# A transformer block kernel: the opening up to the first projection is put in another order

## What is computed

```python
def rms_norm(x, g):
    xf = x.astype(jnp.float32)
    y = xf * lax.rsqrt(jnp.mean(xf * xf, axis=-1, keepdims=True) + NORM_EPS)
    return (y * g.astype(jnp.float32)).astype(x.dtype)
...
mod_x = (silu_c @ w_mod[i] + b_mod[i])[:, None, :]
mod_c = silu_cc @ w_mod[i] + b_mod[i]
sh_x, sc_x, g_x = jnp.split(mod_x, 3, axis=-1)
sh_c, sc_c, g_c = jnp.split(mod_c, 3, axis=-1)
hx = rms_norm(x, norm_g[i]) * (1.0 + sc_x) + sh_x
hc = rms_norm(ctx, norm_g[i]) * (1.0 + sc_c) + sh_c
...
k = px[..., A_WIDTH:A_WIDTH + A_KV_WIDTH]   # px = hx @ w_in
kc = rms_norm(pkv[..., :A_KV_WIDTH] ...)    # pkv = hc @ w_in[:, ...]
```

## Time and profile before

| | us |
|---|---|
| median of 3 runs | 1624.19 (1623.81 to 1627.51) |
| the profiled execution's own time | 1623.98 |
| its span, first to last instruction | 1622.2 |
| TensorE busy | 1534.7 (95% of the span) |
| VectorE, ScalarE, GpSimd busy | 754.4, 640.9, 688.1 |
| mean granted clock of TensorE | 0.978 of full |

### The profile page before, as it was taken

How to read it: one execution, slowest core, us unless ns; L and a number is a source line. 1 busy time by engine, 2 the same in 40 slices (tenths; PEclk the granted TensorE clock), 3 DMA queues, 4 the chain that set the end, 5 groups by cost and what they waited for, 6 DMA issues and landing times.

```text
span 1622.2 us, 25653 instructions
## 1 busy us (share of the span) xinstructions
PE 1534.7 (95%) x10114; PEld 1244.3 (77%) x10114; DVE 754.4 (47%) x1733; ACT 640.9 (40%) x1339; POOL 688.1 (42%) x660
## 2 busy tenths in 40 slices
PE   5999999999899999999998899999999989999997
PEld 3887777777688788787876687878787867766875
DVE  4444555555532534534355454733432564455253
ACT  4234444444532533433334353434332344443331
POOL 2534444443432533433325444535255434444462
PEclk8999999999999999999999999999999999999998
DMA  9111111110233222322321222222131221111221
GB/s 396 44 67 38 42 53 53 53 53 28 72 100 128 78 72 82 108 79 79 105 92 43 100 85 78 79 68 88 52 104 53 92 91 53 53 53 53 94 88 52
DMA packets 22438, 129.80 MB, mean 80 GB/s; under 512 B 2480, under 2 KB 2608, under 8 KB 8368
## 3 DMA queue, kind: packets, MB, share of 16 engines
q1 hardware_dynamic: 22176, 127.92, 22.8%
q10 hardware_dynamic: 144, 0.26, 0.1%
HBM read 126.08 MB, written 2.10 MB: 79 GB/s over the span
## 4 chain that ended last, share of the span: by engine, by line
PE 80%; DVE 9%; ACT 3%; POOL 3%; issue 3%; DMA 1%; SPq 0%; POOLq 0%; DVEq 0%; ACTq 0%
PE PS L1463 15%; PE PS L1465 15%; PE PS L1464 15%; PE PS L1586 6%; PE PS L1561 6%; PE PS L1544 4%; PE PS L1458 3%; PE PS L1459 3%; PE PS L1460 3%; PE PS L1551 3%; DVE sm L2170 2%; PE PS L1639 1%; PE PS L1631 1%; PE PS L1476 1%; DMA XC<-in_xt 1%
## 5 line engine op out<-in xcount | busy, mean ns | idle before, releaser
L2493 POOL TENSOR_TENSOR WL<-W,WH 128x512 fp32r<-128x512 f32 x304 | 400.4, 1332 | 330.9 <-ACT WH L1742 330.6
L1463 PE MATMUL PS<-HX,WH 128*128 128x512 f32 x1008 | 420.3, 417 | 11.8 <-DVE LX L2083 3.9
L1465 PE MATMUL PS<-HX,WL 128*128 128x512 f32 x1008 | 399.1, 396 | 0.0
L1464 PE MATMUL PS<-LX,WH 128*128 128x512 f32 x1008 | 398.2, 395 | 0.0
L1463 PEld LDWEIGHTS PS<-HX,WH 128*128 128x128 f32 x1008 | 193.1, 192 | 62.0 <-issue 17.1
L1465 PEld LDWEIGHTS PS<-HX,WL 128*128 128x128 f32 x1008 | 192.0, 190 | 42.6
L1464 PEld LDWEIGHTS PS<-LX,WH 128*128 128x128 f32 x1008 | 192.7, 191 | 35.8 <-issue 2.6
L1742 ACT CAST WH<-W 128x512 fp32r<-128x512 f32 x320 | 186.8, 618 | 42.0 <-PE PS L1460 25.6
L1830 ACT ACTIVATE AR<-PS,sm 128x768 f32<-128x768 f32 (+4 forms) x160 | 115.7, 723 | 165.2 <-DVE sm L2175 93.7
L2170 DVE TENSOR_REDUCE sm<-PS 128x1 f32<-128x512 f32 (+4 forms) x224 | 149.9, 669 | 43.7 <-PE PS L1551 39.3
L2560 POOL TENSOR_SCALAR AR<-AR,sm 128x768 f32<-128x768 f32 (+1 forms) x96 | 77.1, 804 | 186.2 <-DVE sm L2186 186.0
(11 more groups left out here) (290 smaller groups left out, 2546.3 us busy)
## 6 DMA issues: line engine op xcount, KB each, us to landing
W<-in_wu SPq DMA_DIRECT2D x98, 1024.0 KB, 4.9
AR<-in_wu SPq DMA_DIRECT2D x8, 1024.0 KB, 11.1
AR<-in_biasb SPq DMA_DIRECT2D x32, 256.0 KB, 2.7
XX<-in_xt SPq DMA_DIRECT2D x2, 1024.0 KB, 6.2
out<-XX SPq DMA_DIRECT2D x8, 256.0 KB, 2.2
XX<-in_xt SPq DMA_DIRECT2D x2, 768.0 KB, 5.3
XC<-in_xt SPq DMA_DIRECT2D x1, 1024.0 KB, 14.2
C<-in_cc SPq DMA_DIRECT2D x1, 770.5 KB, 8.7
```

Source lines behind the costliest of these rows:

```text
L1463: e.matmul(o, wh, xh, start=(k == 0), stop=False)
L1464: e.matmul(o, wh, xl, start=False, stop=False)
L1465: t = e.matmul(o, wl, xh, start=False, stop=(k == 7))
L2493: e.tensor_tensor(WL[:, d, a:z], W[:, n % 2, a:z], WH[:, d, a:z].bitcast(F32), ALU.subtract).then_inc(*s_wl_pool.by(n, q))
```

## The change

What it does, part by part:

- SyncE loads x in three pieces (two blocks, two blocks, four blocks) and issues nothing more until the first has landed; the unit W 0 is issued ahead of XC.
- The sums of squares of the context are taken by GpSimd (L2570 after the change), in the plan behind the first two pieces of W 0's low part, which GpSimd now makes too (`helped`). ScalarE writes the eight squares to places of their own (`apart`) and waits for none of the adds.
- The single units 0 and 1 are used and turned ahead of the spread of x's norm, and nothing of the context stands ahead of them.
- The loop is written out: keys of x for blocks 0 and 1 stand behind the use of unit 2, those of blocks 2 and 3 behind unit 4, and so on; one single unit stands between two pieces of keys where two stood.
- The context's blocks are normed later and in groups (3, 2, 3), the high part by ScalarE and the low part by GpSimd in a step of its own (`ctx_low`), and the keys of the context stand two to four blocks behind those of x: blocks 0 and 1 ahead of x's 4 and 5, blocks 2 and 3 ahead of x's 6 and 7, and the last four blocks at the end.
- `Unit("ak", whole=False)`: the keys may start before all four pieces of W 0 are split.

The arithmetic and the number of instructions of each kind stay the same, but for one more load. Behind the opening the order on every engine is the same as before.

```diff
-                split_by[n, q] = "pool" if n > 1 and not quick[0] else "dve"
+                split_by[n, q] = "pool" if (n > 1 or helped[0]) and not quick[0] else "dve"
...
+            def __init__(self, *key, whole=True):
...
-                while any(m <= n for m, _ in pieces):
+                while whole and any(m <= n for m, _ in pieces):
...
         do("early", 1)
+        load(0)
         do("context_load")
-        load(0)
         for n in range(2, 8):
...
-        norm("a", ar, X_CTX, (), lambda k, p: [(s_x[2], (2,)) if p else (s_x[k // 4], (k // 4,))])
+        norm("a", ar, X_CTX, (), lambda k, p: [(s_x[3], (3,))] if p else [(s_x[min(k // 2, 2)], (min(k // 2, 2),))])
+        norms["a"].apart = hb0
...
         norm_sums("a", 0, FIRST)
         next(first[0])
         do("norm_rs", "a", 0)
+        next(first[1])
         WIDE.take("RA", (s_scaled, (0, 7)), (s_rc, (0,)))
-        rbroad("a", 0, PS[:, 0:1024])
-        for k in range(KC):
-            do("square", "a", k, 1)
-        next(first[1])
-        norm_sums("a", 1, FIRST)
+        rdiag("a", 0)
+        split(0)
+        helped[0] = True
+        tick(True)
+        tick(True)
+        helped[0] = False
         run(first[0])
         run(first[1])
+        rspread("a", 0, PS[:, 0:1024])
         for m in range(2):
             for j in range(2):
                 Order.hold(("ak", m, j), (4 + 2 * m + j,), [(s_kraw, (m,))])
-        split(0)
-        for n in range(0, 8, 2):
+        un = Unit("ak", whole=False)
+
+        def first_scale(n):
             do("gain", 0, n)
-            modulate_x(0, n)
-            if n == 0:
-                do("norm_rs", "a", 1)
-                tick(True)
-            modulate_x(0, n + 1)
-            if n < 6:
-                next(first[n + 2])
-                next(first[n + 3])
-            if n == 0:
-                rbroad("a", 1, PS[:, 0:1024])
-                do("scale_ctx", 0)
-                un = Unit("ak")
-            else:
-                keys_rows(1, [n - 2, n - 1])
-            do("scale_ctx_k", 0, n)
-            do("scale_ctx_k", 0, n + 1)
-            if n < 6:
-                run(first[n + 2])
-                run(first[n + 3])
-            keys_rows(0, [n, n + 1])
-        keys_rows(1, [6, 7])
+            do("scale", 0, n)
+            do("scale", 0, n + 1)
+            do("scale_low", 0, n)
+            do("scale_low", 0, n + 1)
+
+        def ctx_norm(*ks):
+            for k in ks:
+                do("ctx_norm", k)
+
+        def ctx_keys(*ks):
+            for k in ks:
+                do("ctx_low", k)
+            keys_rows(1, ks)
+
+        for k in range(KC):
+            do("square", "a", k, 1)
+        first_scale(0)
+        next(first[2])
+        keys_rows(0, [0, 1])
+        next(first[3])
+        tick(True)
+        run(first[2])
+        run(first[3])
+        norm_sums("a", 1, MODS)
+        do("gain", 0, 2)
+        do("scale", 0, 2)
+        do("scale", 0, 3)
+        do("norm_rs", "a", 1)
+        next(first[4])
+        rbroad("a", 1, PS[:, 0:1024])
+        do("scale_ctx", 0)
+        do("scale_low", 0, 2)
+        do("scale_low", 0, 3)
+        ctx_norm(0, 1, 2)
+        tick(True)
+        keys_rows(0, [2, 3])
+        next(first[5])
+        run(first[4])
+        run(first[5])
+        first_scale(4)
+        next(first[6])
+        ctx_keys(0, 1)
+        ctx_norm(3, 4)
+        tick(True)
+        keys_rows(0, [4, 5])
+        next(first[7])
+        run(first[6])
+        run(first[7])
+        first_scale(6)
+        ctx_keys(2, 3)
+        ctx_norm(5, 6, 7)
+        tick(True)
+        tick(True)
+        keys_rows(0, [6, 7])
+        ctx_keys(4, 5, 6, 7)
...
-                if k > 2:
-                    w.wait_ge(*s_acc(name, k - 2, p))
-                o = N.acc if k == 0 else N.sq[(k - 1) % 2]
+                if p and N.apart:
+                    o = N.acc[:, lo:hi] if k == 0 else N.apart.at(k, lo, hi)
+                else:
+                    if k > 2:
+                        w.wait_ge(*s_acc(name, k - 2, p))
+                    o = (N.acc if k == 0 else N.sq[(k - 1) % 2])[:, lo:hi]
                 scale = 1.0 if N.gain is None else v(N.gain, k, k + 1)
-                e.activation(o[:, lo:hi], xT.at(k, lo, hi), ACT.Square, scale=scale).then_inc(*s_sq.by(name, k, p))
+                e.activation(o, xT.at(k, lo, hi), ACT.Square, scale=scale).then_inc(*s_sq.by(name, k, p))
...
+            def square(name, k, p):
+                N = norms[name]
+                if k and p and N.apart:
+                    lo, hi = 128 * N.parts[p][0], 128 * N.parts[p][1]
+                    w.wait_ge(*s_sq(name, k, p))
+                    if k > 1:
+                        w.wait_ge(*s_acc_pool(name, k - 1, p))
+                    e.tensor_tensor(N.acc[:, lo:hi], N.acc[:, lo:hi], N.apart.at(k, lo, hi), ALU.add).then_inc(*s_acc_pool.by(name, k, p))
+
+            def ctx_norm(k):
+                a, h, shift = scaled[0][0], scaled[0][4].at(k, T, NT), mod[0][:, k, 1:2]
+                w.wait_ge(*s_rc(0))
+                w.wait_ge(*s_acc_pool("a", 7, 1))
+                e.tensor_tensor(h, xT.at(k, T, NT), Rc, ALU.mult).then_inc(*s_normed_ctx.by(0, k))
+                w.wait_ge(*s_gain(0, k | 1))
+                w.wait_ge(*s_normed_ctx(0, k))
+                e.tensor_scalar(h, h, a[:, k, 1:2], shift, ALU.mult, ALU.add).then_inc(*s_scaled_ctx.by(0, k))
+
+            def ctx_low(k):
+                w.wait_ge(*s_xh("a", k, 1))
+                e.tensor_tensor(L.at(k, T, NT), scaled[0][4].at(k, T, NT), H.at(k, T, NT).bitcast(F32), ALU.subtract).then_inc(*s_xl_pool.by("a", k, 1))
...
-                for i in range(2):
-                    e.dma_start(XX[:, 2048 * i:2048 * i + 2048], xt[:, 2048 * i:2048 * i + 2048]).then_inc(*s_x[i].by(i))
+                for i, (a, b) in enumerate(((0, 1024), (1024, 2048), (2048, 4096))):
+                    e.dma_start(XX[:, a:b], xt[:, a:b]).then_inc(*s_x[i].by(i))
+                w.wait_ge(*s_x[0](0))
                 e.dma_start(C[:, :], cc).then_inc(*s_c.by())
```

More of the change, by code:

```diff
@@ L266, in build @@
         s_v, s_c, s_cs, s_pos, s_out = (signal(n, 16) for n in ("vectors", "consts", "rope_table", "positions", "stored"))
-        s_x = [signal(f"x{i}", 16) for i in range(3)]
+        s_x = [signal(f"x{i}", 16) for i in range(4)]
         s_w = [signal(f"unit{i}", 16) for i in range(2)]
@@ L350, in build @@
         loaded, unit_end, split_by, split_prev, started = set(), {}, {}, {}, set()
-        pieces, quick, used, part_last = [], [False], [0], [None, None]
+        pieces, quick, helped, used, part_last = [], [False], [False], [0], [None, None]
         groups = {}
@@ L469, in build, with added @@
             sums: object
+            apart: object = None
+            def added(self, name, k, p):
+                return (s_acc_pool if p and self.apart else s_acc)(name, k, p)
         norms = {}
@@ L492, in rbroad, with rdiag, rspread @@
         def rbroad(name, p, o):
+            rdiag(name, p)
+            rspread(name, p, o)
+        def rdiag(name, p):
+            for i in range(*norms[name].parts[p]):
+                dg_prev[name, i], dg_last[i % 4] = dg_last[i % 4], (name, i)
+                do("rdiag", name, i)
+        def rspread(name, p, o):
             rbout[name] = o
             for i in range(*norms[name].parts[p]):
-                dg_prev[name, i], dg_last[i % 4] = dg_last[i % 4], (name, i)
                 do("rbroad", name, i)
@@ L1490, in norm_sums @@
                 w.wait_ge(*s_c())
-                w.wait_ge(*s_acc(name, 7, p))
+                w.wait_ge(*N.added(name, 7, p))
                 lo, hi = N.parts[p]
@@ L1772, in scale @@
                 e.activation(H.at(k, 0, T), hb.at(k, 0, T), ACT.Identity, bias=mod[l][:, k, 0:1]).then_inc(*s_xh.by(phase, k, 0))
-            def scale_ctx_k(l, k):
-                a, Rb, rb, perm, hb, phase, first = scaled[l]
-                w.wait_ge(*s_scaled_ctx(l, k))
-                e.copy(H.at(k, T, NT), hb.at(k, T, NT)).then_inc(*s_xh.by(phase, k, 1))
+            def ctx_norm(k):
+                w.wait_ge(*s_scaled_ctx(0, k))
+                e.copy(H.at(k, T, NT), scaled[0][4].at(k, T, NT)).then_inc(*s_xh.by("a", k, 1))
             def low_ctx_k(l, k):
@@ L1997, in x_gb @@
                 e.activation(sgb[2 * j + m], groups["gb", j, m].out, ACT.Tanh, scale=0.5).then_inc(*s_gbt.by(2 * j + m))
-            program(e, w, dict(silu=silu, split=split, mod_row=mod_row, square=square, scale_ctx=scale_ctx, scale_ctx_k=scale_ctx_k, low_ctx_k=low_ctx_k, scale=scale,
+            program(e, w, dict(silu=silu, split=split, mod_row=mod_row, square=square, scale_ctx=scale_ctx, ctx_norm=ctx_norm, low_ctx_k=low_ctx_k, scale=scale,
                                parts=parts, a_key_raw=a_key_raw, a_key_rope=a_key_rope, a_query_raw=a_query_raw, a_query_high=a_query_high, a_gate=a_gate, score_exp=score_exp,
@@ L2026, in square @@
```

(6 more changed lines are left out.)

21 lines of the change are left out of this document (6 added, 15 removed).

## The result

| | before | changed |
|---|---|---|
| median of 7 runs each, us | 1624.29 (1622.61 to 1627.51) | 1629.82 (1627.40 to 1631.37) |
| ratio, with its 95% interval | | 1.0027 [1.0017, 1.0037] |
| span of the profiled execution | 1622.2 | 1628.6 |
| first matmul of the values, the mark | 62.94 | 67.70 |
| TensorE busy ahead of the mark | 42.27 | 44.96 |

By the ratio the change costs 4.4 us on 1624.19, that is 1628.6 (the medians of the table lie 5.5 apart): just inside "no change", and near the upper end of the range. The change is slower all the same: at the mark the sum gave 0.4, and it is 4.76. Of those, 2.07 are idle time of TensorE and 2.69 the same matmuls taking longer.

A forecast was written before the change was run, and what follows sets the result against it. Bound by TensorE's unchanged work, so only opening waits and clock level count: 1623.98 plus 0.4 at the first values' matmul gives 1624.4, plus 0.3 for GpSimd beside VectorE gives 1624.7 us; range 1619.5 to 1629.5.

The forecast's parts named there:

- the sum: Opening's steps added up to the first values' matmul: 63.3 against 62.94, so 0.4 us slower.
- Where it goes: From first keys to values: lead of 7.1 us shrinks to 2.8 at keys 2 and 3, values at 63.3.
- The loads: Start of the opening: x's last half lands at 8.9, adds end at 12.7 instead of 13.11, gain 0.4 us.
- Holding back the constants costs nothing: Load queue at the start: waiting for x's first piece costs 0, since the constants' bytes come behind x's anyway.
- Up to the first keys: Opening up to keys 0 and 1: they start at 25.1, 7.1 us sooner; GpSimd's adds run 22.1 to 27.9.
- The way to keys 2 and 3: Chain from unit 3 through context's sums and VectorE's diagonals: keys 2 and 3 start at 37.7, 4.3 us sooner.
- Unit 5 44.1, row 44.5, turn 44.8, scaling at 45.6: Hand-offs between keys 2, 3 and keys 4, 5: scaling starts 1.5 us after unit 5 ends.
- The clock: TensorE's low level behind idle time: keys 2 and 3 take 5.4 us, last keys 2.9 plus 1.8.
- What no row shows: GpSimd adding while VectorE makes the first two low parts: VectorE waits at most 0.73 us, 0.3 taken.
- Rival 1: Opening's gaps close: 1620.4 with the high clock, 1617.4 (6.5 us sooner) without waits; chance beyond 4.9 us 0.14.
- Rival 2: GpSimd's adds end late, at 35.7, holding up TensorE's context sums: 7.1 us slower, 1631.1; chance with like delays 0.10.
- Rival 3: Loading x alone at first gains nothing: the 0.4 us goes, 1625.1; counted inside the forecast, no separate chance.

The follow-up runs named there:

- splits_late: Changed kernel with three split pieces issued behind unit 6 instead of ahead of unit 5's row; ratio 1.0005 to the kernel before.
- x_two_wait: Changed kernel with x loaded in two halves, later loads still waiting for the first half to land; ratio 1.0008 to the kernel before.
- adds_vector: Changed kernel with the context's seven adds on VectorE behind the first low parts instead of on GpSimd; ratio 1.0023 to the kernel before.
- late_x_two_fill: Changed kernel with x in two halves, no wait, three splits behind unit 6, and 20 useless matmuls in two TensorE idle places; ratio 0.9982 to the kernel before.
- before_fill: Kernel before with 22 useless matmuls in two of TensorE's idle places; ratio 0.9997 to the kernel before.
- before_x_three: Kernel before with x loaded in three pieces and a wait for the first ahead of other loads; ratio 1.0022 to the kernel before.
- clock_fill: Changed kernel with 32 useless matmuls of 256 columns in four of TensorE's idle times; ratio 1.0008 to the kernel before.
- late_x_two: Changed kernel with x in two halves, no wait, and three split pieces behind unit 6; ratio 0.9990 to the kernel before.

## Why the prediction was where it was

The verdict (within 0.3%, and no gain) came out, but barely, with a centre 4 us too low, and an interval that reaches to 0.37%. Of the signs, the first square (5.37), the first keys and the chain to keys 2 and 3 came as said. The values did not: I had 61 to 65, and 67.70 is just short of the 68 beyond which I had called the mechanism wrong. No set of keys took the full 5.4 either; two ran nine of their twelve at 0.43 and took 4.8. At the mark I had 63.3 and it was 67.70. By the steps of "Where it goes" these 4.4 are:

| stretch | predicted | measured | missing |
|---|---|---|---|
| start to keys 2, 3 | 37.7 | 38.36 | 0.7 |
| keys 2, 3 and unit 5 | 6.4 | 5.07 | -1.3 |
| end of unit 5 to keys 4, 5 | 3.8 | 7.80 | 4.0 |
| keys 4, 5 and unit 7 | 3.9 | 3.84 | -0.1 |
| end of unit 7 to keys 6, 7 | 3.8 | 4.96 | 1.2 |
| keys 6, 7, context's last four | 7.7 | 7.67 | 0.0 |

The 1.3 that keys 2 and 3 gave back is luck of the clock in this execution: they took 4.1 here and 5.3 in splits_late.

- **"The loads" failed.** Its step was "by the rate it lands 2.45 after 6.4, at 8.9", with the 429 GB/s of the earlier trace rows, a window in which larger pieces ran. It landed at 10.24, at 340 to 360 GB/s, and the adds ended at 14.0, not 12.7. "Gain here: 0.4" was a loss of 0.9. "Holding back the constants costs nothing" failed too, as far as the profiles go: x_two_wait has unit 2 at 24.54 against 23.13, and the changed kernel at 24.69 against 24.38 without its wait.
- **"Up to the first keys"** was right in kind: keys at 26.55 against 25.1, late by what the loads were late. The adds ran from 23.01 to 29.5 against 22.1 to 27.9, beside it as said.
- **The way to keys 2 and 3** held, link by link: context's sums 34.25 (32.9), keys 38.36 (37.7), released by VectorE's diagonal.
- **"Unit 5 44.1, row 44.5, turn 44.8, scaling at 45.6" is the step that failed most.** It counted the row's copy and the turn, and left out what the plan puts ahead of them on ScalarE and VectorE: three casts (1.65) and three pieces of WL (2.66). The row was copied 1.9 after unit 5's end and the scaling began 4.7 after it, where I had 1.5. The diff shows one of them (`tick(True)` ahead of `keys_rows(0, [2, 3])`), the order of VectorE all three. The sum has no term for them. That is 3.2 of the 4.0. The other 0.8 is the clock again: "unit 6 and the context's keys 0 and 1 (2.5) lie in this gap", and they took 4.1, past the first low part. The 2.3 from the first scaling to the low part held (48.14 to about 50.4). Of the 1.2 missing ahead of keys 6 and 7, 0.8 lie between unit 7's end and the first scaling (57.38, 2.3 behind it and not 1.5), and 0.4 in the low parts.
- **The clock** was right in sum. I had the low level for all of keys 2 and 3 and it ended after five of them (5.4 became 4.1), and three quarters of the last ones (4.7, measured 4.8). That keys behind such an idle time run at the low level held in part: of the nine kernels of the table that have no useless matmuls ahead of keys 6 and 7, and idle 1.84 to 2.53 there, six took 4.4 to 4.8 for them and three 3.2.
- **"What no row shows"**: I took 0.3, between nothing and one add of 0.73; that VectorE waits at most one add was my estimate, and no run shows the 0.3. adds_vector shows nothing in the time (1.0023 against 1.0027, the intervals overlap). VectorE's first two low parts did take 0.48 longer beside the adds, 1.89 together where adds_vector has 1.41, which is less than one add of 0.73, and unit 2 covered it. The prediction did not look at the other end of the opening: the low parts of blocks 6 and 7, for which the last keys wait, took 2.11 beside GpSimd's context work, where those of blocks 4 and 5 took 1.42. What that is worth was not tried.
- **Rival 1** fell in the changed kernel: the gaps did not close. late_x_two_fill is the nearest to what it describes, with two parts of the change taken back and useless work put in, and gains 1.9 at the mark where it said up to 6.5.
- **Rival 2** fell: the adds ended at 29.5, ahead of the sums. Its result, a loss of some microseconds, came from another place.
- **Rival 3** was right that x alone at first gains nothing, and too mild: it costs.
- Of **the 1.5 us at 110 to 120** nothing was in the prediction, which let the mark set the end. It does not come with the change alone: that turn stands 56.7 to 56.9 behind the mark in the changed kernel and ten of the variants, before_fill and before_x_three among them, and 55.3 in the kernel before, clock_fill and late_x_two_fill. What decides at which level the keys behind the scores run was not tried. It also makes the 6.4 between the two profiled executions more than the 4.4 of the ratio.

Still open: how late_x_two's other ten runs look at the mark; by the time they are 1.6 us under the kernel before. Why x's 512 KB pieces load slower in six of seven executions was not taken further than their size, nor was it tried why unit 2's weights come 1.2 us later with three pieces and no wait. Whether the change's other parts, W 0 ahead of the context or the context's groups, gain or cost was not tried one by one.

## What to carry to other kernels

When a step is moved, list what every engine issues between the link before and the link behind it, and price the queue, not the link alone: here three splits that nobody needed yet cost 3.6 us in a change that lost 4.4. A load cut into smaller pieces is to be priced from a row of such a piece, or its rate left open. And an early start that leaves the rounds of hand-offs as they are moves the idle time behind it: look at how long the last link takes, and at which clock level, before counting the lead as won.
